# Hybrid decoder layer on one core: the squares of both mixers' outputs summed by fp32 products with ones instead of split float32r ones

## The reference, cut to what matters

```python
def mixer_block(hn, pos, w_in, conv_w, a_log, dt_bias, gdn_norm, w_out):
    ...
    o_a = gated_delta_chunked(gq, gk, gv, log_g, beta)
    o_a = o_a * lax.rsqrt(jnp.mean(o_a * o_a, axis=-1, keepdims=True) + EPS) * gdn_norm.astype(f32)
    y_a = (o_a * jax.nn.silu(gz.astype(f32).reshape(B, L, GDN_HEADS, GDN_DV))).reshape(B, L, GDN_V)
    ...
    o_b = retention_chunked(rq, rk, rv.astype(f32).reshape(B, L, RET_HEADS, RET_DV))
    o_b = o_b * lax.rsqrt(jnp.mean(o_b * o_b, axis=-1, keepdims=True) + EPS)
    ...
```

## Time and profile before

| | |
|---|---|
| median of 3 runs | 2281.85 us (2280.13 to 2284.99) |
| the profiled execution, its own time | 2283.06 us |
| its span, first to last instruction | 2281.0 us |
| mean granted TensorE clock | 0.973 |
| instructions | 31938 |
| TensorE matmul rows busy | 2135.6 us, 94% of the span |
| VectorE, ScalarE, GpSimd busy | 1213.4, 680.0, 253.1 us |
| front phase, output phase | to about 1362 us, from about 1377 us |

### The profile page before, as it was taken

How to read it: one execution, slowest core, us unless ns; L and a number is a source line. 1 busy time by engine, 2 the same in 40 slices (tenths; PEclk the granted TensorE clock), 3 DMA queues, 4 the chain that set the end, 5 groups by cost and what they waited for, 6 DMA issues and landing times. The chain is left out here.

```text
span 2281.0 us, 31938 instructions
## 1 busy us (share of the span) xinstructions
PE 2135.6 (94%) x13396; PEld 2055.7 (90%) x13396; DVE 1213.4 (53%) x1427; ACT 680.0 (30%) x863; POOL 253.1 (11%) x259
## 2 busy tenths in 40 slices
PE   7999997689999999899999988899999999999996
PEld 6999997689999999889999988799899898998994
DVE  3434443346555555455443333367667667667666
ACT  4222323324343444333443223231121111212213
POOL 0000002378700212112100000000000000000000
PEclk9999998889999999999999998999999999999998
DMA  6222233444344445334322224101011011011111
GB/s 194 97 91 95 80 124 121 146 141 146 105 149 130 130 135 149 116 97 145 107 93 85 99 70 162 47 28 56 28 55 55 28 55 50 33 55 37 45 37 74
DMA packets 137276, 210.59 MB, mean 92 GB/s; under 512 B 12684, under 2 KB 98260, under 8 KB 137044
## 3 DMA queue, kind: packets, MB, share of 16 engines
q1 hardware_dynamic: 137172, 209.09, 28.4%
HBM read 154.95 MB, written 54.12 MB: 92 GB/s over the span
## 5 line engine op out<-in xcount | busy, mean ns | idle before, releaser
L627 PE MATMUL a_psum<-xh,w_hi 128*128 128x348 f32 x1896 | 622.5, 328 | 1.0 <-DVE w_lo L1059 1.0
L627 PE MATMUL a_psum<-xl,w_hi 128*128 128x348 f32 x1896 | 612.9, 323 | 0.0
L627 PE MATMUL a_psum<-xh,w_lo 128*128 128x348 f32 x1896 | 611.5, 323 | 0.0
L627 PEld LDWEIGHTS a_psum<-xh,w_hi 128*128 128x128 f32 x1896 | 360.4, 190 | 3.4 <-DVE w_lo L1059 1.3
L627 PEld LDWEIGHTS a_psum<-xl,w_hi 128*128 128x128 f32 x1896 | 360.3, 190 | 0.6
L627 PEld LDWEIGHTS a_psum<-xh,w_lo 128*128 128x128 f32 x1896 | 359.7, 190 | 0.0
L928 ACT ACTIVATE post<-a_psum 128x348 f32<-128x348 f32 x234 | 107.6, 460 | 679.6 <-PE a_psum L627 649.8
L134 PE MATMUL c_psum<-c_xh,c_w_hi 128*128 128x342 f32 x1248 | 268.4, 323 | 38.2 <-DVE residual_T L1741 15.7
L1741 DVE TENSOR_TENSOR residual_T<-c_psum,residual_T 128x512 f32<-128x512 f32 x352 | 239.5, 692 | 119.1 <-PE c_psum L1554 119.0
L134 PE MATMUL c_psum<-c_xl,c_w_hi 128*128 128x342 f32 x1248 | 265.6, 321 | 0.0
L134 PE MATMUL c_psum<-c_xh,c_w_lo 128*128 128x342 f32 x1248 | 264.3, 320 | 0.0
(11 more groups left out here) (205 smaller groups left out, 2491.7 us busy)
## 6 DMA issues: line engine op xcount, KB each, us to landing
w_raw<-in_w_in SPq DMA_DIRECT2D x79, 512.0 KB, 3.7
mix_scratch<-post SPq DMA_DIRECT2D x48, 522.0 KB, 2.8
c_w_raw<-in_w_up SPq DMA_DIRECT2D x44, 512.0 KB, 4.6
ext<-mix_scratch SPq DMA_DIRECT2D x9, 1536.0 KB, 8.0
y<-mix_scratch SPq DMA_DIRECT2D x27, 512.0 KB, 6.5
down_raw<-in_w_ffn_down SPq DMA_DIRECT2D x22, 512.0 KB, 3.7
ext<-grow_scratch SPq DMA_DIRECT2D x9, 512.0 KB, 5.5
ext<-mix_scratch SPq DMA_DIRECT2D x9, 512.0 KB, 6.8
```

Source lines behind the costliest of these rows:

```text
L627: mm = pe.matmul(psum[:, u % 2, 0:N3], w[:, k, :], x[:, k, N3 * j:N3 * j + N3], start=(k == 0 and part == 0), stop=(k == KC - 1 and part = ...
```

## The change

The squares go into the products with ones as fp32, with the fp32 ones of the constants. The float32r copy of the ones, both splits, their tiles, semaphores and the `osl` step are gone. The waits that stood on the split's result now stand on the squares (a_rosq, d_z) or, where a buffer's reuse was guarded, on the product that reads it (pe_rss, pe_oss).

```diff
@@ front_plan
             add(("su", c))
             add(("l5r", c + 1))
-        add(("osl", c))
         fill()
         add(("oss", c))
@@ front_phase
-        ones_r = sb("ones_r", [P, P], F32R)
...
-        o_hi, o_lo = sb("o_hi", [P, GH, P], F32R), sb("o_lo", [P, GH, P], F32R)
@@ sync, dl_a
                     elif c == 1:
-                        sp.wait_ge(d_rosl, NCH)
+                        sp.wait_ge(pe_rss, NCH)
@@ tensor
                 elif kind == "r_ss":
                     c = a[0]
-                    pe.wait_ge(d_rosl, c + 1)
+                    pe.wait_ge(a_rosq, c + 1)
                     pe.wait_ge(a_roln, c)
-                    for n, (buf, e) in enumerate(((o_hi, 0), (o_hi, 1), (o_lo, 0), (o_lo, 1))):
-                        mm = pe.matmul(psum[:, 6, :], ones_r[:, :], buf[:, e::2, :], start=(n == 0), stop=(n == 3))
+                    for e in range(2):
+                        mm = pe.matmul(psum[:, 6, :], ones, r_osq[:, e::2, :], start=(e == 0), stop=(e == 1))
                     mm.then_inc(pe_rss, 1)
...
                 elif kind == "oss":
                     c = a[0]
-                    pe.wait_ge(d_osl, c + 1)
+                    pe.wait_ge(d_z, c + 1)
                     if c + 1 < NCH:
                         pe.wait_ge(d_S, 2 * c + 2)
                     for g in range(2):
-                        pe.matmul(psum[:, 6 + g, :], ones_r[:, :], o_hi[:, heads(g), :], start=True, stop=False)
-                        mm = pe.matmul(psum[:, 6 + g, :], ones_r[:, :], o_lo[:, heads(g), :], start=False, stop=True)
+                        mm = pe.matmul(psum[:, 6 + g, :], ones, o_sq[c % 2][:, heads(g), :], start=True, stop=True)
                     mm.then_inc(pe_oss, 1)
@@ scalar
-                    act.activation(ones_r[:, :], ones, ACT.Copy)
...
                     act.activation(r_osq.rearrange("p h c -> p (h c)"), two_banks(4), ACT.Square).then_inc(a_rosq, 1)
-                    act.wait_ge(a_rosq, c + 1)
-                    act.activation(o_hi[:, :, :], r_osq, ACT.Copy).then_inc(a_rosh, 1)
...
                         act.activation(o_ro[:, heads(g), :], four(2 + g), ACT.Square).then_inc(a_osq, 1)
-                    act.wait_ge(d_z, c + 1)
-                    act.wait_ge(pe_oss, c)
-                    act.activation(o_hi[:, :, :], o_sq[c % 2], ACT.Copy).then_inc(a_osh, 1)
@@ vector
-                elif kind == "r_out":
-                    c = a[0]
-                    dve.wait_ge(a_rosh, c + 1)
-                    dve.tensor_tensor(o_lo[:, :, :], r_osq, o_hi[:, :, :].bitcast(F32), ALU.subtract).then_inc(d_rosl, 1)
...
-                elif kind == "osl":
-                    c = a[0]
-                    dve.wait_ge(a_osh, c + 1)
-                    dve.tensor_tensor(o_lo[:, :, :], o_sq[c % 2], o_hi[:, :, :].bitcast(F32), ALU.subtract).then_inc(d_osl, 1)
@@ gpsimd, qk
                     if c >= 2:
-                        pool.wait_ge(d_osl, c - 1)
+                        pool.wait_ge(pe_oss, c - 1)
```

## The result

The changed kernel takes **2295.94 us** (median of 5 runs, 2293.03 to 2298.72) beside 2281.85 us for the kernel before (median of 5, 2279.84 to 2284.99): +14.1 us, a ratio of 1.0060 with a 95% interval of 1.0045 to 1.0074. The forecast was 2293 us within 2287 to 2299, slower. The profiled execution takes 2296.77 us; its span is 2294.8 us.

A forecast was written before the change was run, and what follows sets the result against it. TensorE, busy 94% of the span, was taken to bound the kernel. 14.4 - 0.9 - 0.6 - 1.6 = +11.3 us on the profiled 2283.06 gave 2294.4, less 1.2 for the median: 2293 us, range 2287 to 2299.

The forecast's parts named there:

- Part 1: Products with ones on TensorE: each of 18 sums of squares goes from 0.92 to 1.72 us, +14.4 us.
- Part 2: Dropped casts and subtractions: worth only two TensorE stops, -0.9 us at 707 us and -0.6 us in chunk 8.
- an earlier operand is worth 0: Products outside the two stops: L703 and L846 start with no idle time, so getting operands earlier gains 0.
- Part 3: Longer product taken up where TensorE waits for ScalarE's chain anyway, in chunks 2 and 5 of the delta loop: -1.6 us.
- no second loss: Chunk 3: Ln waits for the product, so its chain moves 0.8 us with TensorE; no gain and no further loss.
- so the 2.9 us wait at 600 us stays: Retention loop: Ln, VectorE's L1172, the convolution and w_lo move by TensorE's same 0.8 us, leaving this wait unchanged.
- Part 4: Waits of SyncE, GpSimd, r_ss and oss, moved to other operands: each costs 0; no DMA added or moved.
- the clock adds about 3.4 us to either side: Low-clock stretches after waits near 600, 950 and 995 us: moved stops can lose or gain such a stretch.
- B: Rival: 41 us less in two in-order queues removes TensorE's waits and low-clock stretches, faster, 2270 us; chance 0.04.
- C: Rival: an fp32 matmul costs as much as its split, so the products add 0, 2280 us; chance 0.03.
- D: Rival: nothing taken up; delays in ScalarE's and VectorE's chains make two more stops with clock stretches, 2303 us; chance 0.11.

The follow-up runs named there:

- the split kept: fp32 products of the changed kernel, but casts, subtractions and the waits on them as before; +16.2 us, ratio 1.0071 against the kernel before.
- Retention alone: Kernel before with only retention's sums of squares in fp32 without the split; +3.2 us (1.0014), again +3.7 us (1.0016) against the kernel before.
- the delta rule alone: Kernel before with only the delta rule's sums of squares in fp32 without the split; +4.8 us, ratio 1.0021 against the kernel before.
- the halves added in fp32: Changed kernel, but in retention VectorE first adds a head's two halves, one fp32 matmul replacing two; +6.9 us (1.0030) against the kernel before.
- halves added and then split: Kernel before with retention's halves added by VectorE, then split: two float32r matmuls instead of four; -2.5 us (0.9989) against the kernel before.
- every product twice: Changed kernel with each product with ones made twice into the same bank, in retention and delta rule; +37.0 us (1.0162) against the kernel before.

## Why the prediction was right or wrong

**Part 1, right.** The term that decides was +14.4 us: 18 sums, each 0.80 us longer. All four records of a sum start 0.43 us apart, at 512 columns as extrapolated from 348 and 256, and twice as many of them keep that distance. Where no wait lies between, the start of one sum follows the last 29.3 us later instead of 28.5 in retention and 40.1 instead of 39.3 in the delta rule: 0.8 us more. The reading of the Trainium skill's "Perfetto Trace Analysis", section "Engine Utilization", that would have made this term 0 fell with them. Another page of the Trainium skill, "FP8 and Floating Point Precision", section "TensorE Precision Notes", states four passes for true fp32; the trace agrees: two records at 0.43 us are close to four times 0.213 us, 512 columns at 2.4 GHz.

**Part 2, right in place, somewhat small in size.** Both stops went. But the stop in `r_st` is not one of 0.86 us: the second profile of the kernel before has two, with the split kept there are three. The term was 1.5 us and measures 1.4, 2.1 and 2.4 in these three profiles. That elsewhere "an earlier operand is worth 0" holds for the products themselves, but dropping the split did more than that near 600 us: the wait there is 2.8 us with fp32 products and the split kept (one profile), and 2.3 in both profiles of the changed kernel.

**Part 3, right in two chunks of the delta rule, wrong at 600 us and probably in chunk 3.** In chunk 2 the wait for Ln is gone, but the wait for k and q behind it is 4.8 and 4.6 us in the two profiles of the changed kernel where the two before have 4.1 and 4.0. Retention alone, with the delta rule as before, has 4.0 and 4.7, so that wait varies by itself. Over the whole distance from the sum of chunk 2 to that of chunk 3 the kernel before takes 47.2 and 48.1 us and the changed kernel 48.3 and 47.7, so the 0.8 us was taken up on average, within this scatter. In chunk 5 the wait for k and q went from 2.76 us to 2.07, and from 2.87 to 2.17 in the second profiles, near the 0.8 of the forecast.

In chunk 3 Ln waited longer for the product, as said (0.46 us before):

```profile
991.16 1.11 ACT L1029 ACTIVATE post<-a_psum,a_cst 128x1024 f32<-128x1024 f32 x1 [1.26 <-PE a_psum L843]
```

But "no second loss" is not what the profiles show there. The wait of 4.13 us for VectorE that follows (L737, now L734) is the same before and after. Behind it, though, the changed kernel has a lower clock. The first 5 us after that wait, kernel before, then changed:

```profile
998.45:1003.45 5.00, 5.00 (x26) 5.00 (x27) 4.30 (x12) 0.00 (x0) 1.26 (x1) 0.66 0.91 261
```

```profile
1009.68:1014.68 5.00, 5.00 (x22) 5.00 (x22) 4.29 (x12) 0.00 (x0) 1.11 (x1) 0.50 0.91 263
```

From the end of that wait to the sum of chunk 4 it takes 26.6 us instead of 25.7, in both profiles of each kernel. Retention alone has 25.7 too, twice; the delta rule alone, the split kept and the halves added in fp32 have 26.4 to 26.8. So chunk 3 cost about 1.7 us and not 0.8 in every profile that makes the delta rule's sums in fp32 once. But two others don't fit: with halves added and then split, the delta rule as before, it is 27.0, and with every product twice 25.7. That the longer sum lowers the clock there is likely and not shown.

The step that failed in retention is the sentence that everything moves by the same 0.8 us, "so the 2.9 us wait at 600 us stays". It was 2.3 us in both profiles of the changed kernel and of retention alone, and 1.2 with every product made twice. VectorE's queue sets it. In the kernel before, then in the changed one, the scaling of o and the convolution behind it:

```profile
591.82 1.23 DVE L1172 TENSOR_TENSOR y<-a_psum,y 128x1024 f32<-128x1024 f32 x1 [1.61 <-ACT y L979]
592.96 0.95 DVE L1117 TENSOR_SCALAR post<-post,a_par 128x1040 f32<-128x1040 f32 x1
593.95 6.20 DVE L1121 SCALAR_TENSOR_TENSOR post<-post,a_par 128x1040 f32<-128x1040 f32 x3
```

```profile
593.64 1.22 DVE L1158 TENSOR_TENSOR y<-a_psum,y 128x1024 f32<-128x1024 f32 x1 [2.41 <-ACT y L972]
594.78 1.82 DVE L1107 TENSOR_SCALAR post<-post,a_par 128x1040 f32<-128x1040 f32 x1
596.64 4.77 DVE L1111 SCALAR_TENSOR_TENSOR post<-post,a_par 128x1040 f32<-128x1040 f32 x3
```

From the start of the scaling to the start of the operation that TensorE waits for (L1161, now L1151) VectorE takes 10.49 us before and 9.92 after, 0.57 us less, and TensorE's wait went from 2.88 to 2.31 us, 0.57 less. GpSimd works beside the convolution, and the two queues did not move by the same time. Counted from the start of the chunk's sum, the scaling starts 3.3 us later instead of 2.7, but GpSimd's operation of 1024 columns (L1369, now L1351) 3.7 instead of 5.3. So VectorE meets GpSimd at another point, and its convolution takes 0.5 us less. The second profiles of both kernels and both of retention alone give the same lengths within 0.02 us; with the split kept it is 10.37 us and a wait of 2.76.

**Part 4, right.** No wait of TensorE is for the moved ones.

**The sum.** Predicted +11.3; measured +14.1 and +11.4 in two comparisons, whose intervals (10.3 to 16.9 and 8.0 to 14.8 us) both hold the forecast and overlap, so their difference needs no cause. The first profile of the changed kernel shows 3.7 instead of 2.5 us at 790 us and 0.89 instead of 1.00 of clock over 30 us, but the second profiles have it the other way round. This was in the range as "the clock adds about 3.4 us to either side". In part the sum is right by luck: it leaves out a loss of 0.9 us in chunk 3, and against that the 0.6 us at 600 us and up to 0.9 us by which the stops of part 2 were larger.

**The rivals.** B, the freed engines win: the split kept costs only 2 to 5 us more, so all that they freed is worth that much. C fell with the first row of the products. D, new stops: no new stop and no longer one is of the change's making, but the lower clock in chunk 3, 0.9 us, would be a cost of D's kind if it follows from the change.

## What to carry to other kernels

Where TensorE sets the time, price a change of number format in its matmuls first: four float32r matmuls of 512 columns took 0.92 us here and two fp32 ones 1.72, whatever that takes off the other engines. Over the eleven comparisons (a line through 0 by least squares has the slope 0.83) a microsecond of TensorE work was worth about 0.8 us. That number rests mostly on the version with every product twice; the small ones scatter from 0.4 to 1.1, with intervals of about 3 us each. Some waits shrink when TensorE is slower and grow when it is faster, but not all. And a delay that reaches VectorE's queue but not GpSimd's changes where the two meet, and with it a wait of TensorE. For terms of a few us, take two profiles of the same kernel before a wait or a clock stretch is put down to an edit.

## What the runs showed of the hardware

**The order of VectorE and GpSimd decides the longer wait.** The wait near 790 us hangs on three convolution operations of VectorE beside two of GpSimd. With GpSimd idle, three of them take 3.98 us (at 768.70 us in the kernel before), 1.3 us each. Kernel before, first profile, then second profile:

```profile
778.75 5.52 DVE L1121 SCALAR_TENSOR_TENSOR post<-post,a_par 128x1040 f32<-128x1040 f32 x3
...
780.22 5.84 POOL L1405 TENSOR_TENSOR ext<-a_cst 128x1024 f32<-128x1024 f32 x2 [45.98 <-DMA a_cst<-xt_scratch]
```

```profile
779.24 7.20 DVE L1121 SCALAR_TENSOR_TENSOR post<-post,a_par 128x1040 f32<-128x1040 f32 x3
...
780.53 4.81 POOL L1405 TENSOR_TENSOR ext<-a_cst 128x1024 f32<-128x1024 f32 x2 [46.09 <-DMA a_cst<-xt_scratch]
```

GpSimd starts 1.47 us after VectorE's first operation in the one and 1.29 us in the other; VectorE's three take 5.52 or 7.20 us, and GpSimd's two 5.84 or 4.81. The profiles of the changed kernel give both cases too: 7.18 us in the first, 5.52 in the second. Since VectorE's second operation is due some 1.3 us after the first, 0.2 us decides whether it or GpSimd's is first, and who is second waits. All 13 profiles fit: in the ten where GpSimd starts 1.43 us or more after VectorE's first operation, VectorE's three take 5.5 us and TensorE waits 1.6 to 2.6 us; in the three where it is 1.26 to 1.29 us, they take 7.2 us and TensorE waits 3.7 to 4.5. The Trainium skill says in "SBUF — State Buffer", section "Who interferes with whom", that a VectorE instruction with two SBUF inputs contends with a GpSimd instruction that reads SBUF, and that issue order decides who blocks. The trace agrees, with 1.7 us of VectorE's time gained or lost by it.

**The clock after a wait.** Behind the same wait, at 2.5 us the clock over 780 to 810 us was 1.00 and at 3.7 and 4.5 us it was 0.89. At 1.7 us, in the second profile of the changed kernel, it was 0.94:

```profile
780.00:810.00 30.00, 28.35 (x198) 27.50 (x198) 18.56 (x17) 11.44 (x15) 12.86 (x5) 0.94 0.65 205
```

So a shorter wait does not always keep the clock. Nor does the same wait always cost the same: behind 2.88 us near 600 us, in code that does not differ up to there, the clock over 596 to 616 us was 0.83, 0.83 and, with the delta rule's half alone, 1.00. What a wait costs can't be told from its length alone.
